# Seven-product form for the projections that feed the scan, in both layers

## The reference

```python
ql, kl, vl, zl, xbcl, dtfl, dtbl, gal, gsl = in_proj_split(h_l @ w_in)      # latent tokens
qc, kc, vc, zc, xbcc, dtfc, dtbc, gac, gsc = in_proj_split(h_c @ w_in)      # context tokens
xs_c, bm_c, cm_c, dtf_c, dtb_c = ssd_inputs(xbcc, ...)   # depthwise conv of 5 taps + silu; dt = softplus
xs_l, bm_l, cm_l, dtf_l, dtb_l = ssd_inputs(xbcl, ...)
yc_f, st_f = ssd_chunked(xs_c, dtf_c, a_f, bm_c, cm_c, h0, with_ctx_out)    # forward, chunks of 128 tokens
yl_f, _    = ssd_chunked(xs_l, dtf_l, a_f, bm_l, cm_l, st_f, True)          # and the same backward
ssd_l = rmsnorm((yf + yb + ssd_d * xs) * silu(z), g) @ w_ssd_o
```

## Time and profile before

| | |
|---|---|
| median of 3 runs | 2700.45 us (2700.17 to 2704.59) |
| the profiled execution | 2700.33 us |
| its span | 2698.5 us |
| mean granted TensorE clock | 0.997 |
| TensorE busy | 2669.2 us, 99% |
| VectorE busy | 1292.7 us, 48% |
| ScalarE busy | 761.9 us, 28% |
| GpSimd busy | 622.5 us, 23% |

### The profile page before, as it was taken

One profiled execution on the slowest core, in us unless ns is written; L12 is line 12 of the kernel. 1 busy time (PEld: TensorE's weight loads), 2 busy tenths in 40 slices (PEclk: granted clock), 3 DMA queues, 4 the chain that ended last, 5 costly groups with the idle time before them and its releaser, 6 DMA issues.

```text
span 2698.5 us, 33892 instructions
## 1 busy us (share of the span) xinstructions
PE 2669.2 (99%) x13090; PEld 1984.5 (74%) x13090; DVE 1292.7 (48%) x2279; ACT 761.9 (28%) x1740; POOL 622.5 (23%) x534
## 2 busy tenths in 40 slices
PE   8999999999999999999999999999999999999999
PEld 6778885555555666788778888866666777888887
DVE  1432234778778334787668451146677523212101
ACT  2430002656656333100022110015545422101100
POOL 4000000223323122275424454403122122000000
PEclk9999999999999999999999999999999999999999
DMA  9356666434342221233355432264344222567552
GB/s 264 96 160 194 187 194 171 106 103 110 91 111 66 55 55 39 63 110 103 100 160 184 142 92 87 86 168 126 104 115 111 79 71 65 155 188 210 153 151 78
DMA packets 518992, 330.62 MB, mean 123 GB/s; under 512 B 15296, under 2 KB 485680, under 8 KB 518832
## 3 DMA queue, kind: packets, MB, share of 16 engines
q1 hardware_dynamic: 507600, 296.10, 38.7%
q0 software_dynamic: 10784, 31.46, 4.7%
q10 hardware_dynamic: 448, 0.89, 0.1%
HBM read 327.06 MB, written 1.34 MB: 122 GB/s over the span
## 4 chain that ended last, share of the span: by engine, by line
PE 93%; DVE 2%; issue 2%; ACT 1%; PEld 1%; POOL 0%; DMA 0%; DVEq 0%; PEldq 0%; POOLq 0%; ACTq 0%
PE ps L1266 43%; PE ps L1646 23%; PE ps L1802 4%; PE ps L1814 3%; PE ps L1793 3%; PE ps L1955 3%; PE ps L1777 2%; PE ps L1916 1%; PE ps L1754 1%; PE ps L1939 1%; PE ps L1587 1%; PE ps L1928 1%; PE ps L2032 1%; PE ps L1292 0%; PE ps L1740 0%
## 5 line engine op out<-in xcount | busy, mean ns | idle before, releaser
L1266 PE MATMUL ps<-xnT,W 128*128 128x256 f32 (+1 forms) x2912 | 901.3, 468 | 2.2 <-DVE TMP L2409 0.9
L1266 PEld LDWEIGHTS ps<-xnT,W 128*128 128x128 f32 x2912 | 549.6, 190 | 320.0 <-issue 257.9
L1266 PE MATMUL ps<-BIG,W 128*128 128x256 f32 x1440 | 315.0, 379 | 0.0
L1266 PEld LDWEIGHTS ps<-BIG,W 128*128 128x128 f32 x1440 | 272.6, 190 | 37.1 <-issue 0.4
L1646 PE MATMUL ps<-TMP,W 128*128 128x256 f32 x1192 | 273.3, 379 | 0.0
L1646 PEld LDWEIGHTS ps<-TMP,W 128*128 128x128 f32 x1192 | 226.5, 190 | 30.8
L1646 PE MATMUL ps<-BIG,W 128*128 128x256 f32 x1016 | 230.5, 379 | 0.0
L803 ACT ACTIVATE TMP<-ps 128x512 f32<-128x512 f32 (+5 forms) x172 | 89.5, 528 | 440.9 <-PE ps L1646 209.6
L1646 PEld LDWEIGHTS ps<-BIG,W 128*128 128x128 f32 x1016 | 192.8, 190 | 27.1 <-issue 1.0
L2409 DVE SCALAR_TENSOR_TENSOR TMP<-ps,prmT,TMP 128x510 f32<-128x510 f32 (+3 forms) x256 | 181.6, 714 | 42.6 <-ACT TMP L1002 27.8
L2445 DVE SCALAR_TENSOR_TENSOR TMP<-TMP 128x128 f32<-128x128 f32 x384 | 162.4, 494 | 41.6 <-ACT TMP L1038 41.6
(11 more groups left out here) (350 smaller groups left out, 3002.5 us busy)
## 6 DMA issues: line engine op xcount, KB each, us to landing
W<-in_w_in SPq DMA_DIRECT2D x188, 512.0 KB, 4.0
W<-in_w_mlp SPq DMA_DIRECT2D x128, 512.0 KB, 4.0
W<-in_ada_w SPq DMA_DIRECT2D x96, 512.0 KB, 4.0
BIG<-cs_rows POOLq DMA_DIRECT2D x96, 256.0 KB, 4.7
W<-in_w_ssd_o SPq DMA_DIRECT2D x32, 512.0 KB, 3.6
W<-in_w_gate SPq DMA_DIRECT2D x22, 512.0 KB, 5.1
W<-in_w_up SPq DMA_DIRECT2D x22, 512.0 KB, 3.9
W<-in_w_down SPq DMA_DIRECT2D x16, 512.0 KB, 3.8
```

Of the source, the lines that this page charges most:

```text
L1266: last = mm(dst, w[:, c, 0:m], rhs(k), start=k == 0, stop=k == total - 1)
```

## The change

The pairs x0/x1, B/C and z0/z1 of layer 0 and the pair x0/x1 of layer 1 are made by `quick`. These are 32 units: 24 at the head of `QUICK` and 8 at its end.
- Their banks are 0, 1, 4 and 5; the last two are those of the transposed x.
- The combined projections lie in SBUF: x and z in `yz`, B and C in `zs`. ScalarE's `center` and `gated` and VectorE's `conv` read them there. `decayed` reads `xc`, the copy of the transposed x in SBUF, which is now made first (both banks, in layer 1 too).
- GpSimd makes the weight sums of 32 more units (`weights_summed`, four instructions each), VectorE 32 combinations and one set of token sums for each layer, kept in a new tensor `TX`. In the merge of layer 0 `ga` and `gs` use those of the scan, and three sets of token sums fall away there.
- The ring gets 12 slots a group in layer 0 instead of 6, 8 in layer 1.
- The first token sums stand ahead of the dt chain on VectorE, dt ahead of the first projection on TensorE, and the first weight sums ahead of the `cs_rows` store on GpSimd.
- `cs_rows` is stored in another order of rows, so that one DMA broadcasts a chunk for both directions.
- VectorE's masks of chunk 1 in layer 0 stand ahead of the combination of x.
- The sums for f1 are made in one go, into `TX`.
- The scratch for DMA descriptors is set to 8192.

The diff, cut to its core:

```diff
+PARTS = {"x0": ("x0", "x1"), "bc0": ("B", "C"), "z0": ("z0", "z1"), "x1": ("x0", "x1")}
+QUICK = [(x, g, 0) for g in range(NG) for x in ("x0", "bc0", "z0")]
+M0 = len(QUICK)
...
+END20 = len(QUICK) - 1
+QUICK += [("x1", g, 0) for g in range(NG)]
...
-        TMP = sb("TMP", [P, 13000])
+        TMP = sb("TMP", [P, 12800])
+        TX = sb("TX", [P, 4, 4, S])
...  GpSimd
+                for j in PRELUDE[l]:
+                    weights_summed(j)
+                pool.wait_ge(dt_dve, 9 * l + 7)
...
                         if g < NG - 1:
                             broadcast(g + 1, i)
+                        if l == 0 and i == 1 and g < NG - 1:
+                            weights_summed(unit("bc0", g + 1))
+                            weights_summed(unit("z0", g + 1))
+                    if g < NG - 2:
+                        weights_summed(unit(f"x{l}", g + 2))
...  TensorE, quick
+                if ph in PARTS:
+                    pe.wait_ge(dt_dve, 9 * int(ph[-1]) + 1)
+                    pe.wait_ge(ssd["xc"], ssd_first["xc"] * int(ph[-1]) + n)
                 give(seventh(bank_c, 0, w1, 0, t1, opens=True), k1)
...  TensorE, turned
-                    if g:
-                        R("xcd", 3 * g)
-                        R("xc", g)
+                    pe.wait_ge(q_rel, 3 * quick_group(last_unit(g)) + 3)
...  TensorE, the scan
                     if more:
-                        front(g + 1, 0)
+                        x_unit = quick_steps(unit(f"x{l}", g + 1))
+                        for _ in range(4):
+                            next(x_unit)
                     states(g, 0)
                     states(g, 1)
                     if more:
-                        front(g + 1, 1)
-                        if l == 0:
-                            front(g + 1, 4)
+                        for _ in x_unit:
+                            pass
...
-                    if more:
+                    if more and l == 0:
+                        quick(unit("bc0", g + 1))
+                    elif more:
                         front(g + 1, 2)
                         front(g + 1, 3)
...  VectorE, conv and decayed
-                    raw = PS[t % 2][:, 0:n].rearrange("p (s n) -> p s n", n=S)
+                    raw = (kept_tile(l, g, t) if is_quick(l, t) else PS[t % 2][:, 0:n]).rearrange(...)
-                                               PS[4 + ch // 2][:, (ch % 2) * S:(ch % 2) * S + S]
+                                               xc[:, ch, :].rearrange("p (h e) -> p h e", e=HD),
...  VectorE, the scan of one group
+                    R("tr", 3 * g + 3)
+                    if g:
+                        R("ychunk", n_ch * g)
+                    for b in range(2):
+                        last = V.tensor_copy(flat(xc[:, 2 * b:2 * b + 2, :]), PS[4 + b][:, :])
+                    last.then_inc(ssd["xc"], 1)
...
                     decayed(g, 2)
+                    if l == 0:
+                        masked(g, 1)
                     if more:
+                        combined(unit(f"x{l}", g + 1))
+                    dve.drain()
+                    carried(g, 1)
+                    if l and more:
+                        masked(g, 1)
                         conv(g + 1, 0)
...
                     if l == 0:
                         masked(g, 2)
+                        if more:
+                            combined(unit("bc0", g + 1))
                         masked(g, 3)
                     if more:
                         conv(g + 1, 2)
                         conv(g + 1, 3)
...
+                    if more and l == 0:
+                        combined(unit("z0", g + 1))
...
-    nc = bacc.Bacc("TRN2", target_bir_lowering=False, num_devices=1)
+    nc = bacc.Bacc("TRN2", target_bir_lowering=False, num_devices=1, dynamic_dma_scratch_size=8192)
```

More of the change, by code:

```diff
@@ L312, in weight_tiles @@
             at = (SSD_X + g * 256, SSD_X + P + g * 256, SSD_B + g * P, SSD_C + g * P, SSD_Z + g * 256, SSD_Z + P + g * 256)
-            for t in front_order(l, g):
+            if g == 0:
+                col(("dt", l), wi, SSD_DT, 64)
+            for t in range(6):
                 col(("ssd", l, g, FRONT[t]), wi, at[t])
-                if g == 0 and t == 0:
-                    col(("dt", l), wi, SSD_DT, 64)
+                if t % 2 and (l == 0 or t == 1):
+                    tiles += [(key, []) for key in quick_keys(unit(f"{('x', 'bc', 'z')[t // 2]}{l}", g))[2:]]
         for h in range(8):
@@ L991, in wide_of, with first_kept, whole_of @@
                     return T if t < 3 else n_tok
+                def first_kept(j):
+                    ph, n, _ = QUICK[j]
+                    act.wait_ge(q_p2, j + 1)
+                    if ph == "bc0" and n >= 2:
+                        R("y1", 2 * (n - 2) + 2)
+                    if ph == "z0":
+                        R("conv", 4 * n + 2)
+                    if ph in ("ga", "gs", "so", "ao") and n:
+                        act.wait_ge(m_free, 2 * n)
+                    if ph == "wout20":
+                        act.wait_ge(m_free, 8)
+                    copy(kept_at(j)[:, 0:S], PS[quick_banks(quick_group(j))[0]][:, 0:S]).then_inc(q_p1, 1)
+                def whole_of(g, t):
+                    act.wait_ge(q_rel, 3 * quick_group(unit(f"{('x', 'bc', 'z')[t // 2]}{l}", g)) + 3)
+                    return kept_tile(l, g, t)
                 def center(g, t):
-                    made(act, ("ssd", l, g, FRONT[t]))
+                    if not is_quick(l, t):
+                        made(act, ("ssd", l, g, FRONT[t]))
                     if g:
@@ L1112, in _ @@
                         decays(g, 2)
+                        if more:
+                            first_kept(unit("bc0", g + 1))
                         decays(g, 3)
@@ L1191, in _ @@
                 if l == 0:
-                    for j in range(F10 - 3):
+                    for j in range(M0, F10 - 3):
                         if quick_last(j):
@@ L1830, in _ @@
                 ada_columns(*GAP["f20" if l else "down1"])
-                front(0, 1)
-                front(0, 2)
+                quick(unit(f"x{l}", 0))
+                if l == 0:
+                    after = quick_steps(unit("bc0", 0))
+                    for _ in range(3):
+                        next(after)
+                else:
+                    front(0, 2)
                 pe.wait_ge(dt_dve, 9 * l + 3)
                 for c in range(2):
-                    last = nc.tensor.transpose(PS[5][:, c * P:(c + 1) * P], xb[:, c * P:(c + 1) * P], ident)
+                    last = nc.tensor.transpose(PS[3][:, c * P:(c + 1) * P], xb[:, c * P:(c + 1) * P], ident)
                 last.then_inc(dt_pe, 1)
@@ L1839, in _ @@
                 last.then_inc(dt_pe, 1)
-                front(0, 3)
+                if l == 0:
+                    for _ in after:
+                        pass
+                else:
+                    front(0, 3)
                 pe.wait_ge(dt_act, 5 * l + 3)
@@ L1853, in _ @@
                 mm(PS[3][:, 0:256], ones, flat(tot), start=True, stop=True).then_inc(dt_pe, 1)
-                for t in range(4, 6):
-                    front(0, t)
+                if l == 0:
+                    quick(unit("z0", 0))
+                else:
+                    for t in range(4, 6):
+                        front(0, t)
                 pe.wait_ge(dt_dve, 9 * l + 9)
@@ L1892, in _ @@
                         next(head0)
+                    elif l == 0:
+                        z_unit = quick_steps(unit("z0", g + 1))
+                        for _ in range(4):
+                            next(z_unit)
                     outputs(g, 1 if l else 3)
+                    if more and l == 0:
+                        for _ in z_unit:
+                            pass
                     if more:
@@ L2057, in _ @@
                     ada_columns(*GAP["wout20"])
-                    for j in range(F10, len(QUICK)):
+                    for j in range(F10, END20 + 1):
                         quick(j)
@@ L2733, in _ @@
                     k = sums_job(F10)
-                    sums_of_f10 = tokens_summed(k)
-                    for _ in range(3):
-                        next(sums_of_f10)
+                    all_summed(k)
                     sums("f10", 0)
-                    made(dve, ("f10", 0, 1))
-                    for _ in sums_of_f10:
-                        pass
                     adds(*GAP["wout20"])
```

404 lines of the change are left out of this document (228 added, 176 removed).

## The result

The changed kernel takes **2842.35 us** (median of 4 runs, 2838.13 to 2845.99), the kernel before 2700.31 beside it: a ratio of 1.0523, interval 1.0504 to 1.0542. Slower was right; 2781 was 61 us too low, and 2842 lies outside the range.

A forecast was written before the change was run, and what follows sets the result against it. VectorE, slowed by its lock with GpSimd, was to become the bound of layer 0. 2700.3 us + 47 (layer 0) + 25 (layer 1) + 9 (before the first group) = 2781 us; range 2690 to 2815.

The forecast's parts named there:

- The saving of the form: TensorE, scan: 1.64 us less a unit; groups of 46.4 us (layer 0) and 36.8 (layer 1) if TensorE set the pace.
- VectorE keeps up: Rival, layer 0: GpSimd's sums run while VectorE reads PSUM or waits; TensorE leads at 46.4 us, 2675 us whole; chance 0.12.
- The price of a hit: VectorE's SBUF-only instructions: each GpSimd TENSOR_TENSOR starting beside them costs 1.01 us; instructions reading PSUM pay nothing.
- whole-instruction rule: Lock held for the whole instruction: a hit costs 1.26 us, layer 0 period 61.4, total 23 us higher; not adopted.
- The other rule: PSUM source costs VectorE 62 cycles more than SBUF: conv's move would gain 1.0 us a group, 7 in all; not booked.
- The number of hits: Layer 0 group: 13 of 20 GpSimd instructions hit VectorE, near today's share of 5 in 8; bounds 5 and 20.
- My loop: VectorE's loop in a layer 0 group: 45.0 us before any lock, 58.1 with 13 hits, against TensorE's 46.4.
- The hand walk: Layer 0: walking through the new order gave 16 hits, with the next x half's sums on a combination.
- VectorE as the bound: Layer 0: VectorE's loop of 58.1 us against TensorE's 46.4 sets the period, 6.8 us more a group, +47 us.
- Layer 1: Layer 1 periods: z products wait for conv of B, 39.0 us plus 3 hits makes 42.0; +25 us over 7 periods.
- Before the first group: Ahead of each layer's first group: token sums delay the dt chain, early weight sums hit it; +6 and +3, together +9 us.
- The clock: Rival, layer 0: granted clock falls while TensorE waits; below 0.80 TensorE leads again; at 0.75, 2808 us; chance 0.03.

The follow-up runs named there:

- e4: Changed kernel with the five additions of each scan combination and GpSimd's scan weight sums both cut to 2 columns; 2716.6 us.
- e11: Changed kernel, scan weight sums cut to 2 columns; in layer 1 z products moved to banks 4 and 5, last carried state ahead of convolution 0; 2714.0 us.
- e1: Changed kernel with GpSimd's weight sums of all 32 scan units cut to 2 columns of 128; 2739.8 us.
- e3: Changed kernel with the five additions of each scan combination cut to 2 columns, weight sums whole; 2821.1 us.
- e6: Changed kernel with the broadcasts of the decay rows issued by ScalarE's own queue, behind the exponentials; 2835.6 us.
- e7: e4 plus 10 idle TensorE products ahead of the second outputs of a layer 0 group and of the z products of a layer 1 group; 2741.4 us.
- e8: e7 with fewer idle products, 5 in layer 0 and 4 in layer 1; 2721.7 us.
- e2: Kernel before with 12 (layer 0) and 4 (layer 1) more GpSimd additions a group, on a buffer nobody reads; 2720.7 us.

## Why the prediction was right and wrong

**The saving of the form.** Right as work: 46.54 and 36.70 us (e4) against 46.4 and 36.8 forecast. Wrong as a period: "If TensorE still set the pace" had no loop in it. With sums and combinations both out, layer 0 still takes 49.5 us (e4), which leaves 1.8 of the 4.9 us, and layer 1 takes 40.1, more than before. In layer 1 that is order: a unit delivers its two tiles only at its end, and with the two moves the period is 36.63 us (e11). In layer 0 TensorE comes for masks 2 sooner than they are ready; how much of that is order and how much the hits that remain is open. The rival "VectorE keeps up" at 46.4 us did not come even with both costs out.

**The price of a hit.** Right. Besides the masks' 1.01 us, single lines of VectorE in layer 0 show it, min/median/max in ns:

```profile
L2588 DVE SCALAR_TENSOR_TENSOR TMP<-BIG,prmT,TMP x96: 740/750/1793, 576.9 to 918.4; 128x508 f32<-128x508 f32 x48, 128x510 f32<-128x510 f32 x48
L2601 DVE TENSOR_TENSOR TMP<-TMP x36: 408/416/1492, 553.1 to 880.3; 128x256 f32<-128x256 f32 x36
L2628 DVE TENSOR_TENSOR TMP<-TMP x24: 691/693/1729, 561.1 to 912.2; 128x512 f32<-128x512 f32 x24
```

1793 - 740, 1492 - 408, 1729 - 691: 1.04 to 1.08 us each. The whole-instruction rule of the Trainium skill (SBUF — State Buffer, section "SBUF: two separate sides") would, as I read it, make each the 1.26 us of the addition; these three lines don't show that. The other rule of the Trainium skill that I weighed (VectorE: DVE Perf Modes, section on the TRN2 errata) would have made conv cheaper from SBUF: the median above is 750 ns, and the mean before 747 from PSUM, so it doesn't show either, and the zero that I booked stands.

**The number of hits: the step that failed most.** The forecast was 61 us too low: 30.6 of them in the periods of layer 0, 16.1 in those of layer 1, 13.2 in the two beginnings, 1.2 in the rest. In layer 0 the step is the count: I took 13 hits of 20. VectorE's busy time without the sums is 47.0 us, which is my own work of 42.2 (43.7 without the 1.5 between instructions) and about 5 hits; the sums add 12.6 us on the middle periods, so 17 to 18 hits. By line, over the time alone, the same periods show 12.8 us in the masks, 1.0 in their additions, 3.3 in conv and 1.7 in the decays. My loop with 17.5 hits gives 45.0 + 17.7 = 62.7 us; those middle periods took 63.5 on the mean, all seven 62.39. That this is so close is partly luck: with the sums out the same loop gives 50.0 us where e1 took 52.0. The 13 came from today's share (5 in 8). But today's share belongs to today's order, with conv and decays that read PSUM and masks of one chunk at a time beside the sums; after the change 11 of 12 weight additions hit in the group shown, nearly all on masks, and the other products hit conv. The hand walk (16) knew it and was nearer; its one free place, the sums of the next x on a combination, did not happen either: the second of those additions comes 5.8 us late, on masks 3 (786.59, below).

**VectorE as the bound.** Right for the changed kernel (busy for 93% of a period, TensorE for 82%, forecast over 90% and about 80%), wrong as a rule for what a part costs. By my sum a microsecond of VectorE's work is a microsecond of the period; the cut of the combinations takes 5.4 us of its work out of a group and shortens the period by 2.5 (e3, e4). The period is a chain through masks, outputs and convolutions, in which VectorE has most of the time: 49.5 for TensorE and the waits on the way, 2.5 for the combinations, 10.4 for the sums. The hits of the sums stand almost wholly in it because they fall on the masks, which TensorE awaits.

**Layer 1.** +25 forecast, +41 measured. The wait of z for conv of B was called and is there, but I let carried 2 pass, which stood behind conv 0 and made the outputs wait another 3.2 us. The 3 hits were about right (2.5 us of VectorE's busy time, 1.9 of the period). And the first period costs 9.6 us more than before, not 5: there TensorE also waits 3.6 us for GpSimd's last weight sum.

**Before the first group.** +6 and +3 forecast, 12.65 and 9.5 measured (the second from layer 0's last start of the transposes to layer 1's first). In layer 0 12.0 of it goes with the sums, which hit token sums and softplus chain (I had put "a few times"): the two last 23.4 us together and 15.4 in e1. The other 4 us of the 12 were not traced. In layer 1 the sums play no part (9.0 of the 9.5 us remain in e1): there TensorE waits 2.0 us for the combination behind the dt chain and 3.8 us for conv, the z products behind the second wait run at a granted clock of 0.73 (9.7 us), and the dt products take 5.6 us instead of 3.7, which stays open.

**The clock.** Forecast as a rival only below 0.80. It is at 0.87 to 0.94 in layer 0, and TensorE's busy time is 50.9 us there instead of 46.5. It falls where TensorE waits; how much of these 4.4 us reaches the period was not separated.

**The range.** The case that happened, 17 to 18 hits, was within my bounds (5 to 20), and it alone makes +79 in layer 0 (62.7 less 51.35, seven times); with layer 1 and the two beginnings also at their upper side the sum is above 2815. I had cut the range where all four terms had to be high at once, though one cause (work that comes late for TensorE) can drive them together.

## What to carry to other kernels

Before two engines are summed up separately, follow one result through the group: a form that saves products but delivers its tiles late can lose its saving in a loop that was closed to the microsecond (layer 1), and an engine that gets faster comes too early for what others make (layer 0). If a helper engine's instructions contend with another engine's, count how much of the latter's work is exposed after the change, not before. And the place to use such a form is where nobody waits for the result soon: one unit a group, for the gates, gained 0.24%; all 32 lost 5%.

## What the runs showed of the hardware

**A drain on GpSimd behind a DMA that it has issued waits for microseconds.** GpSimd's timeline in the changed kernel:

```profile
778.63 0.91 POOL L774 DMA_DIRECT2D BIG<-cs_rows  x1
779.56 1.27 POOL L786 TENSOR_TENSOR W<-W 128x512 f32<-128x512 f32 x1
786.59 1.39 POOL L788 TENSOR_TENSOR W<-W 128x512 f32<-128x512 f32 x1 [5.76 <-issue]
```

```profile
758.25 1.30 POOL L786 TENSOR_TENSOR W<-W 128x512 f32<-128x512 f32 x1
759.70 1.39 POOL L788 TENSOR_TENSOR W<-W 128x512 f32<-128x512 f32 x1
```

With a broadcast ahead of it, the addition behind the drain starts 5.76 us after the first ended; in the unit at 758.25, with no DMA ahead, at once. With the broadcasts on ScalarE's queue nearly all such waits were gone (e6). What exactly the drain awaits was not tried. The Trainium skill (SBUF — State Buffer, section "SBUF: two separate sides") says that GpSimd can't write the descriptors of its DMA while VectorE runs an operation in a two-port mode; the waits were there in e1 too, with the additions cut to 2 columns, and no run here separates VectorE's part.

**A wait of about 2 us can cost a second time through the granted clock**, and not always: in e4 the z products of layer 1 took 8.86 us behind a wait of 2.12 us and 7.17 behind one of 2.03 us. With idle products in this wait the clock stayed at 1.00 (e7, e8). In layer 0 of e8 it stayed at 1.00 although waits of up to 2.2 us were left.

**Costs were additive** (10.36 and 10.37; 2.51 and 2.52) on a loop in which no engine was busy throughout. The agreement to a hundredth is luck: each mean is of one execution, whose periods differ by some us.

**Which of VectorE's inputs lie in SBUF decides whether conv can be hit.** Sixteen conv instructions a group took 11.9 us with a PSUM input, in the kernel before and in e2 with 12 more additions beside them, and 15.1 us with both inputs in SBUF (changed kernel and e1).
